# Gated linear attention in a two-layer transformer block: a later wait for the matrix, and the last heads' norm taken by PSUM banks

## The chip, the cores and the metric

The kernel runs on one core of one Trainium2 chip. The metric is the device time of one execution in microseconds. Five engines share the work: TensorE (PE) multiplies matrices into PSUM, VectorE (DVE) and ScalarE (ACT) work element by element, GpSimd (POOL) does what is left over, and SyncE (SP) issues most transfers. They run their own instruction streams and wait for one another through semaphores.

## The reference

Two layers of a transformer block over 1,024 latent and 256 context tokens, all in fp32. Each layer mixes the tokens in three ways (gated linear attention, differential attention, sliding-window attention), projects the mix, and runs a feed-forward block. The change concerns the first of the three, with 4 heads of 64 channels, computed forwards and backwards, summed, and closed by a norm and a gate:

```python
def gla_output(o, og, g):
    bsz, nh, n, dv = o.shape
    on = rms_norm(jnp.moveaxis(o, 1, 2), g)          # x * rsqrt(mean(x^2) + eps) * g, per head
    return (on * jax.nn.silu(og.reshape(bsz, n, nh, dv))).reshape(bsz, n, nh * dv)
...
        gla_lat = gla_output(ol_f + ol_b, pl['go'], gla_norm_g[layer])
```

Layer 0 needs the result for context and latent tokens, layer 1 for the latent ones alone.

## The kernel before, in words

`gated_linear_attention` (from L1284) runs once a layer as a phase of its own; a phase ends when all five instruction streams have ended, and the next (differential attention, from L2236) begins behind it. The 1,280 tokens are 10 chunks of 128 columns; `ASKED` are the chunks whose output is wanted: all 10 in layer 0, the 8 latent ones (2 to 9) in layer 1. One PSUM bank holds 512 columns, four chunks, so the chunks 0 to 3, 4 to 7, and 8 to 9 lie in three banks.

TensorE's work is a list of *units* (`order`, L1345 to L1364), each filling one of the two slots of the PSUM tensor `U` (three banks each) in turn. For each head: transposed keys, the diagonal, the states, seven *levels* of a block-wise attention matrix, and the output. Each entry names the engine that empties the unit, and `slot` (L1505) lets TensorE begin a unit when the unit before the last has been emptied. ScalarE copies the levels 0 and 1 into the matrix `A`, VectorE the diagonal and, under a mask, the levels 2 to 6 (L1790). `S` holds the states, one for each chunk and direction (L1780).

`output(h)` on TensorE (L1555) waits until ScalarE has copied level 1 and VectorE level 6, that is, until `A` is whole; then it clears the unit by a product with zeros (L1561), adds the state products of both directions (L1568, L1575), and last the products of `A` with the values (L1580):

```python
            def output(h):
                s = slot(("output", h))
                pe.wait_ge(act_took, taken(("level", h, 1)))
                pe.wait_ge(dve_took, taken(("level", h, len(LEVELS) - 1)))
```

The heads are normed in pairs. For a pair `i`, ScalarE copies the second head's output out of PSUM into `out` (L1658) and squares it (L1702); TensorE takes the mean of the squares over each head's 64 rows, two columns for each chunk (`mean`, L1588); ScalarE takes the root (L1696), VectorE the reciprocal (L1800); TensorE spreads each reciprocal over 64 rows and the chunk's columns (`root`, L1597); VectorE, which has multiplied `out` by the gate meanwhile (L1796), multiplies it by the spread (L1805); SyncE stores the pair (L1443). For pair 0 all this stands among head 2's levels. For pair 1 nothing is left to stand beside it. `DP` are two further banks, used by the distances (L1501, L1502) until head 3's levels. Every fp32 matmul of the program is two instructions in the profile.

The next phase starts with the score products of its first head (L2349), whose operands were loaded during gated linear attention; VectorE there first waits for the landing of both stores (`gla_stored`, L2514).

Of the kernel before, what the change touches and what calls it, by code (L numbers as in the profile page):

```python
# [18 lines left out]
ALU = mybir.AluOpType  # L19
ACT = mybir.ActivationFunctionType  # L20
AX = mybir.AxisListType

P = 128
# [1260 lines left out]
def gated_linear_attention(nc, t, res, layer, tiles):  # L1284


    with nc.cleanup_on_exit(), ExitStack() as ctx:
# [47 lines left out]
        unit_done, act_took, dve_took, bank_left = sem("unit_done"), sem("act_took"), sem("dve_took"), sem("bank_left")  # L1335
        silu_done, gate_ready, squared, rs_done, og_done = (
            sem("silu_done"), sem("gate_ready"), sem("squared"), sem("rs_done"), sem("og_done"))
        block = ctx.enter_context(nc.Block())
        proj = t["proj"]
        order, taker = [], []  # L1340

        def plan(name, engine, takes):
            order.append(name)
            taker.append((engine, takes))
        for g in range(NS):  # L1345
# [10 lines left out]
            else:  # L1356
# [3 lines left out]
                    plan(("mean", 0), "act", 1)  # L1360
                if h == 2 and p == 4:
                    plan(("root", 0), "dve", 1)
        for name, engine in ((("output", H - 1), "act"), (("mean", 1), "act"), (("root", 1), "dve")):
            plan(name, engine, 1)  # L1364
        at = {name: n for n, name in enumerate(order)}

        def taken(name):
            engine = taker[at[name]][0]
            return sum(k for e, k in taker[:at[name] + 1] if e == engine)

        def left(name):
            return sum({"keys": 1, "diagonal": 1, "output": 4}.get(x[0], 0) for x in order[:at[name]])

        def made(name):
            return at[name] + 1
# [29 lines left out]
        def chunk(c):  # L1405
            return slice(c * P, (c + 1) * P)
# [6 lines left out]
        @block.sync  # L1413
        def _(sp):
            def gates(h):
                load_gates(sp, t, h, ghi[h % 2][:, :, :], glo[h % 2][:, :, :], g_in[h])

            def keys_and_queries(h):
                load_keys_and_queries(sp, t, h, kq[h % 2], kq_in[h % 2])

            sp.dma_start(V[:, :, :], t["vals"][0:T, V_GLA:V_GLA + 2 * P].rearrange("(c p) f -> p c f", p=P)).then_inc(load["v"], 16)
            sp.dma_start(masks[:, :, :], t["gla_masks"]).then_inc(load["mask"], 16)
            sp.dma_start(block_mean[:, :], t["block_mean"]).then_inc(load["bm"], 16)
            for half in range(2):
# [12 lines left out]
            load_differential_constants(sp, t, res["early"], layer)  # L1437
            load_differential_queries(sp, t, res["early"]["queries"], tiles[0] * P, res["early"]["q_in"])
            for h in range(EARLY_HEADS):
                load_differential_keys(sp, t, res["early"]["keys"][:, 2 * h:2 * h + 2, :], h, res["early"]["k_in"][h])  # L1440
            for i in range(2):
                sp.wait_ge(dve_took, taken(("root", i)))
                sp.dma_start(t["mix"][i * P:(i + 1) * P, t0:], out[:, i, t0:]).then_inc(stored, 16)  # L1443

        @block.gpsimd
# [41 lines left out]
        def _(pe):  # L1487
# [66 lines left out]

            def output(h):  # L1555
                s = slot(("output", h))
                pe.wait_ge(act_took, taken(("level", h, 1)))
                pe.wait_ge(dve_took, taken(("level", h, len(LEVELS) - 1)))
                rows = slice(HALF * (h % 2), HALF * (h % 2) + HALF)
                for t0, tn in ((0, BANK), (BANK, BANK), (2 * BANK, T - 2 * BANK)):  # L1560
                    pe.matmul(U[:, s, t0:t0 + tn], zero[:, 0:P], zero[:, 0:tn], start=True, stop=False, skip_group_check=True)  # L1561
                fence = left(("output", h))
                for k in range(NA):
                    f, b = C0 + k, C0 + (k + NA // 2) % NA
                    if f in (4, 8):
                        pe.wait_ge(bank_left, fence + ((2 if C0 else 1) if f == 4 else 3))
                    if f > 0:
                        mm = pe.matmul(U[rows, s, chunk(f)], S[UP, h % 2, f, :], XAB[UP, h % 2, 0, chunk(f)],  # L1568
                                       start=False, stop=False, skip_group_check=True)
                        if f in (3, 7):  # L1570
                            mm.then_inc(bank_left, 1)
                    if b in (C0, 4):
                        pe.wait_ge(bank_left, fence + ((1 if C0 else 2) if b == C0 else 4))
                    if b != 1:
                        mm = pe.matmul(U[rows, s, chunk(b)], S[DOWN, h % 2, BACK.index(b), :], XAB[DOWN, h % 2, 1, chunk(b)],  # L1575
                                       start=False, stop=False, skip_group_check=True)
                        if b in (7, 9):
                            mm.then_inc(bank_left, 1)
                for c in ASKED:
                    mm = pe.matmul(U[rows, s, chunk(c)], V[:, c, h * HALF:(h + 1) * HALF], A[:, h % 2, c, :], start=False, stop=True, skip_group_check=True)  # L1580
                mm.then_inc(unit_done, 1)

            def mean(i):
                s = slot(("mean", i))
                pe.wait_ge(squared, i + 1)
                pe.wait_ge(load["bm"], 16)
                for c in ASKED:
                    mm = pe.matmul(U[:, s, 2 * c:2 * c + 2], square[:, chunk(c)], block_mean[:, 0:P:HALF], start=True, stop=True)  # L1588
                mm.then_inc(unit_done, 1)

            def root(i):
                s = slot(("root", i))
                pe.wait_ge(rs_done, i + 1)
                for c in ASKED:
                    for half, rows in enumerate((UP, DOWN)):
                        spread = rs[:, i, 2 * c + half:2 * c + half + 1].to_broadcast([P, HALF])
                        mm = pe.matmul(U[rows, s, chunk(c)], spread, ident[:, :], start=True, stop=True)  # L1597
                mm.then_inc(unit_done, 1)
# [31 lines left out]
                        root(0)  # L1630
                distances(g + 2, 4)
            output(H - 1)
            mean(1)
            root(1)

        @block.scalar
        def _(act):
# [17 lines left out]
            def take_output(h):  # L1655
                act.wait_ge(unit_done, made(("output", h)))
                rows = slice(HALF * (h % 2), HALF * (h % 2) + HALF)
                act.activation(out[rows, h // 2, t0:], U[rows, at[("output", h)] % 2, t0:T], ACT.Copy, scale=0.125).then_inc(act_took, 1)  # L1658
# [48 lines left out]
            for g in range(NS):  # L1707
# [21 lines left out]
                if h == 0 and p == 4:  # L1729
                    act.wait_ge(load["go"], 16)  # L1730
                    act.activation(go[:, :, :], go[:, :, :], ACT.Silu).then_inc(silu_done, 1)
            take_output(H - 1)
            squares(1)
            take_mean(1)

        @block.vector
        def _(dve):
# [70 lines left out]
            for g in range(NS):  # L1808
# [24 lines left out]
                    reciprocals(0)  # L1833
                if h == 2 and p == 4:
                    take_root(0)
            gate_output(1)
            reciprocals(1)
            take_root(1)

# [1613 lines left out]
```

## Time and profile before

| | us |
|---|---|
| median of 3 runs | 3616.13 (3611.66 to 3618.82) |
| profiled execution, own time | 3619.33 |
| its span in the trace | 3617.4 |
| TensorE busy | 3397.8 (94%) |
| mean granted TensorE clock | 0.967 of full speed |

All times in the rows are microseconds from the start of the span, unless marked ns. The granted clock is 1.00 at 2.4 GHz and 0.50 at 1.2 GHz. In a row of the timeline, `x20` are twenty instructions merged, and the bracket gives the engine's idle time before them and who ended it. PE is TensorE's products, SPq a transfer issued by SyncE.

### The profile page before, as it was taken

The numbers are of one execution on the slowest core, as the hardware profiler recorded it, in microseconds if no ns is written. First come the engines' busy times: TensorE is split into PE (matmuls) and PEld (weight loads), VectorE is DVE, ScalarE is ACT, GpSimd is POOL, SyncE is SP. The second block draws the span as 40 slices with busy tenths as digits, with TensorE's granted clock in tenths as the row PEclk, the third lists the DMA queues.
The fourth block names the chain that finished last, engine by engine and source line by source line (L and its number), as shares of the span: only waits on it lengthen the run. The fifth ranks groups of instructions, "written<-read, shape, count | busy, mean of one in ns | idle before, by whom it ended". The sixth has DMA issues, their size and how long they took to land. (4 is left out here: it accounts for less than half of the span.)

```text
span 3617.4 us, 52096 instructions
## 1 busy us (share of the span) xinstructions
PE 3397.8 (94%) x20432; PEld 2812.0 (78%) x20432; DVE 1643.0 (45%) x2521; ACT 1463.9 (40%) x2355; POOL 1671.9 (46%) x1017
## 2 busy tenths in 40 slices
PE   4999897989999999999999999888898999999998
PEld 4988885666688888888888888886666788888886
DVE  4046545856553322125443317548665441225534
ACT  4151764855443311113343342658654442222222
POOL 3111443943444444445666211338634365556654
PEclk8999996999999999999999999999999999999999
DMA  5244421266532121223333335521455323233322
GB/s 213 88 138 162 123 52 52 53 175 201 168 110 72 64 93 64 70 65 105 122 108 102 112 118 181 151 47 55 96 187 163 111 93 124 98 99 122 106 99 88
DMA packets 207488, 402.54 MB, mean 111 GB/s; under 512 B 19840, under 2 KB 114400, under 8 KB 206752
## 3 DMA queue, kind: packets, MB, share of 16 engines
q1 hardware_dynamic: 185200, 373.88, 32.7%
q10 hardware_dynamic: 20480, 21.32, 1.8%
q0 software_dynamic: 1584, 4.24, 0.4%
q8 instruction: 155, 2.54, 0.3%
q14 instruction: 69, 0.57, 0.0%
HBM read 328.06 MB, written 71.32 MB: 110 GB/s over the span
## 5 line engine op out<-in xcount | busy, mean ns | idle before, releaser
L2907 POOL TENSOR_TENSOR ffn_wlo<-ring_raw,ffn_whi 128x1024 fp32r<-128x1024 f32 x130 | 330.7, 2546 | 306.0 <-ACT ffn_whi L2764 305.7
L2907 POOL TENSOR_TENSOR outproj_ffn_wlo<-ring_raw,outproj_ffn_whi 128x1024 fp32r<-128x1024 f32 x130 | 329.7, 2538 | 303.9 <-ACT outproj_ffn_whi L2764 303.9
L3160 DVE TENSOR_TENSOR ffn_silu<-banks,ffn_silu 128x512 f32<-128x512 f32 x110 | 70.1, 637 | 608.6 <-PE banks L135 608.6
L133 PE MATMUL banks<-second_uhi,ffn_whi 128*128 128x512 f32 (+1 forms) x880 | 325.2, 370 | 1.4 <-POOL ffn_wlo L2907 1.4
L133 PE MATMUL banks<-second_uhi,outproj_ffn_whi 128*128 128x512 f32 (+1 forms) x880 | 324.6, 369 | 2.0 <-PEq L398 2.0
L134 PE MATMUL banks<-second_ulo,ffn_whi 128*128 128x512 f32 (+1 forms) x880 | 324.4, 369 | 0.0
L135 PE MATMUL banks<-second_uhi,ffn_wlo 128*128 128x512 f32 (+1 forms) x880 | 324.2, 368 | 0.0
L134 PE MATMUL banks<-second_ulo,outproj_ffn_whi 128*128 128x512 f32 (+1 forms) x880 | 323.9, 368 | 0.0
L135 PE MATMUL banks<-second_uhi,outproj_ffn_wlo 128*128 128x512 f32 (+1 forms) x880 | 323.7, 368 | 0.0
L2764 ACT CAST ffn_whi<-ring_raw 128x1024 fp32r<-128x1024 f32 x132 | 138.0, 1048 | 325.0 <-PE banks L135 211.8
L2764 ACT CAST outproj_ffn_whi<-ring_raw 128x1024 fp32r<-128x1024 f32 x130 | 135.9, 1049 | 328.1 <-PE banks L135 193.0
L2772 ACT ACTIVATE ffn_silu<-banks 128x512 f32<-128x512 f32 x110 | 61.0, 555 | 456.5 <-PE banks L135 455.8
L2488 DVE TENSOR_SCALAR_CACHE_REDUCE diff_scores<-diff_scores 128x1280 f32<-128x1280 f32 (+1 forms) x144 | 196.7, 1383 | 24.1 <-PE diff_scores L2349 19.2
L3176 DVE TENSOR_TENSOR y<-banks,y 128x512 f32<-128x512 f32 x200 | 138.1, 691 | 133.6 <-PE banks L135 133.6
L2466 POOL TENSOR_TENSOR diff_w<-diff_w,diff_e 128x1280 f32<-128x1280 f32 (+1 forms) x72 | 192.0, 2667 | 6.0
L2022 POOL TENSOR_SCALAR swa_p<-swa_p,swa_rden 128x640 f32<-128x640 f32 (+1 forms) x144 | 107.3, 763 | 189.0 <-DVE swa_rden L2204 189.0
L2418 ACT ACTIVATE diff_e<-diff_scores,diff_negmax 128x1280 f32<-128x1280 f32 (+1 forms) x144 | 178.2, 1238 | 37.6 <-DVE diff_scores L2488 36.8
L133 PEld LDWEIGHTS banks<-second_uhi,outproj_ffn_whi 128*128 128x128 f32 x880 | 165.9, 189 | 30.3 <-issue 2.8
L133 PEld LDWEIGHTS banks<-second_uhi,ffn_whi 128*128 128x128 f32 x880 | 166.3, 189 | 29.6 <-POOL ffn_wlo L2907 1.8
L135 PEld LDWEIGHTS banks<-second_uhi,ffn_wlo 128*128 128x128 f32 x880 | 166.2, 189 | 27.9
L134 PEld LDWEIGHTS banks<-second_ulo,ffn_whi 128*128 128x128 f32 x880 | 166.4, 189 | 27.4
L135 PEld LDWEIGHTS banks<-second_uhi,outproj_ffn_wlo 128*128 128x128 f32 x880 | 165.9, 188 | 27.7
(375 smaller groups left out, 8892.7 us busy)
## 6 DMA issues: line engine op xcount, KB each, us to landing
ring_raw<-w_ffn_dram SPq DMA_DIRECT2D x264, 512.0 KB
swa_ada_w<-w_ada_dram SPq DMA_DIRECT2D x20, 2048.0 KB
local_qhl<-heads_scratch SPq DMA_DIRECT2D x36, 256.0 KB, 8.3
outproj_mix<-mix_scratch SPq DMA_DIRECT2D x18, 512.0 KB, 4.5
first_ada_w<-w_ada_dram SPq DMA_DIRECT2D x4, 2048.0 KB
outproj_wraw<-w_out_dram SPq DMA_DIRECT2D x8, 1024.0 KB, 9.7
in_w_raw<-w_in_dram SPq DMA_DIRECT2D x15, 512.0 KB, 5.7
heads_scratch<-in_vAhi SPq DMA_DIRECT2D x12, 640.0 KB, 3.0
```

The source lines that it names most:

```text
L133: pe.matmul(out, st_hi, mv_hi, start=start, stop=False)
L134: pe.matmul(out, st_hi, mv_lo, start=False, stop=False)
L135: return pe.matmul(out, st_lo, mv_hi, start=False, stop=stop)
L2022: pool.tensor_scalar(pr[:, m % RING, j, 0:keys], pr[:, m % RING, j, 0:keys], rden[:, m % RING, j:j + 1], 1.0, ALU.mult, ALU.mult).then_inc ...
L2418: act.activation(E[:, r % 4, c, 0:keys], SC[:, c, 0:keys], ACT.Exp, bias=ng[:, c:c + 1], scale=-1.0, accum_out=den[:, c, tile_of(i, r), r ...
L2466: pool.tensor_tensor(w, w, E[:, u % 4, 0, 0:keys], ALU.add).then_inc(w_done, 1)
L2488: dve.tensor_scalar(SC[:, c, 0:keys], SC[:, c, 0:keys], -scale, 3e38, ALU.mult, ALU.min, accum_out=ng[:, c:c + 1]).then_inc(neg_done, 1)
L2764: act.copy(whi(w), raw[:, w % 2, :]).then_inc(w_hi, 1)
L2772: act.activation(sg[:, n % 2, 0:tn], GT[:, n % 2, 0:tn], ACT.Silu).then_inc(silu_done, 1)
L2907: pool.tensor_tensor(wlo(w), raw[:, w % 2, :], whi(w).bitcast(F32), ALU.subtract).then_inc(w_ready, 1)
L3160: dve.tensor_tensor(sg[:, n % 2, 0:tn], UP[:, n % 2, 0:tn], sg[:, n % 2, 0:tn], ALU.mult).then_inc(mul_done, 1)
L3176: dve.tensor_tensor(Y(tt)[:, cols], accumulators(q, n)[:, half, :], Y(tt)[:, cols], ALU.add).then_inc(y_added, 1)
```

## The change

It has three parts. `output(h)` waits for the states before it clears the unit, and for `A` behind the state products. The last head's output and the second pair's norm are taken out of the unit order and done by banks: `BY_BANK` holds the asked chunks of each bank (4, 4, 2 in layer 0; 2, 4, 2 in layer 1), and copy, square, mean, root, gate, reciprocal, spread and scaling are each issued three times on these parts, interleaved by hand on each engine, with six new semaphores. The means go to the two banks of `DP`, the spreads to the other slot of `U`. ScalarE takes a root of one column of constants ahead of the last copies. The store waits for the third scaling and stays one transfer.

```diff
+        BY_BANK = [[c for c in ASKED if c * P // BANK == n] for n in range(3)]
+        plan(("output", H - 1), "act", len(BY_BANK))
-        for name, engine in ((("output", H - 1), "act"), (("mean", 1), "act"), (("root", 1), "dve")):
-            plan(name, engine, 1)
...
+        sums, spreads = U[:, at[("output", H - 1)] % 2, :], U[:, 1 - at[("output", H - 1)] % 2, :]
@@ SyncE
-                sp.wait_ge(dve_took, taken(("root", i)))
+                if i == 0:
+                    sp.wait_ge(dve_took, taken(("root", 0)))
+                else:
+                    sp.wait_ge(scaled, len(BY_BANK))
@@ TensorE, output(h)
                 s = slot(("output", h))
-                pe.wait_ge(act_took, taken(("level", h, 1)))
-                pe.wait_ge(dve_took, taken(("level", h, len(LEVELS) - 1)))
+                pe.wait_ge(dve_took, taken(("states", h)))
...
-                for c in ASKED:
-                    mm = pe.matmul(U[rows, s, chunk(c)], V[...], A[:, h % 2, c, :], ...)
-                mm.then_inc(unit_done, 1)
+                pe.wait_ge(act_took, taken(("level", h, 1)))
+                pe.wait_ge(dve_took, taken(("level", h, len(LEVELS) - 1)))
+                for part in BY_BANK:
+                    for c in part:
+                        mm = pe.matmul(U[rows, s, chunk(c)], V[...], A[:, h % 2, c, :], ...)
+                    if h == H - 1:
+                        mm.then_inc(weighed, 1)
+                if h < H - 1:
+                    mm.then_inc(unit_done, 1)
+            def last_mean(n):
+                pe.wait_ge(squared, n + 2)
+                if n == 2:
+                    pe.wait_ge(rooted, 1)
+                for k, c in enumerate(BY_BANK[n]):
+                    mm = pe.matmul(DP[:, n % 2, 2 * k:2 * k + 2], square[:, chunk(c)], block_mean[:, 0:P:HALF], ...)
+                mm.then_inc(mean_done, 1)
+            def last_spread(n):
+                pe.wait_ge(inv_done, n + 1)
+                for c in BY_BANK[n]:
+                    for half, rows in enumerate((UP, DOWN)):
+                        mm = pe.matmul(spreads[rows, chunk(c)], rs[:, 1, 2 * c + half:2 * c + half + 1].to_broadcast([P, HALF]), ident[:, :], ...)
+                mm.then_inc(spread_done, 1)
...
             output(H - 1)
-            mean(1)
-            root(1)
+            last_mean(0); last_mean(1); last_spread(0); last_mean(2); last_spread(1); last_spread(2)
@@ ScalarE
-            take_output(H - 1)
-            squares(1)
-            take_mean(1)
+            def last_output(n):
+                cols = columns(BY_BANK[n])
+                act.wait_ge(weighed, n + 1)
+                act.activation(out[DOWN, 1, cols], sums[DOWN, cols], ACT.Copy, scale=0.125).then_inc(act_took, 1)
+                act.wait_ge(act_took, taken(("output", H - 1)) - len(BY_BANK) + n + 1)
+                act.activation(square[:, cols], out[:, 1, cols], ACT.Square).then_inc(squared, 1)
+            def last_root(n):
+                act.wait_ge(mean_done, n + 1)
+                act.activation(sd[:, 1, heads_of(part)], DP[:, n % 2, 0:2 * len(part)], ACT.Sqrt, bias=eps[:, 0:1]).then_inc(rooted, 1)
+            act.activation(sd[:, 1, 0:1], eps[:, :], ACT.Sqrt)
+            act.wait_ge(unit_done, made(("mean", 0)))
+            last_output(0); last_output(1); last_root(0); last_output(2); last_root(1); last_root(2)
@@ VectorE
-            gate_output(1)
-            reciprocals(1)
-            take_root(1)
+            last_gate(n):    wait squared n + 2;  out *= go on the bank's columns             -> og_done
+            last_inverse(n): wait rooted n + 1;   rs = 1 / sd on the bank's columns           -> inv_done
+            last_scaling(n): wait spread_done n + 1, og_done n + 2; out *= spreads            -> scaled
+            last_gate(0); last_gate(1); last_inverse(0); last_gate(2); last_inverse(1)
+            last_scaling(0); last_inverse(2); last_scaling(1); last_scaling(2)
```

The calls in a row stand on lines of their own in the kernel, and VectorE's three functions are given by what they wait for and do.

## Rows read from the trace of the kernel before

**Rows 1.** The page: busy time of each engine, share of the span, instructions.
```profile
PE 3397.8 (94%) x20432; PEld 2812.0 (78%) x20432; DVE 1643.0 (45%) x2521; ACT 1463.9 (40%) x2355; POOL 1671.9 (46%) x1017
```

**Rows 2.** Timeline, layer 0's end: start us, us, engine, line, operation, out<-in, count [idle before].
```profile
545.47 1.60 DVE L1790 COPY_PREDICATED gla_A<-gla_masks,gla_unit 128x1280 f32<-128x1280 int32 x1 [0.29 <-PE gla_unit L1552]
...
547.75 0.28 PE L1552 MATMUL gla_unit<-gla_X,gla_XK 128*128 128x128 f32 x1
548.06 1.57 DVE L1790 COPY_PREDICATED gla_A<-gla_masks,gla_unit 128x1280 f32<-128x1280 int32 x1 [1.00 <-PE gla_unit L1552]
549.78 0.82 PE L1561 MATMUL gla_unit<-gla_zero 128*128 128x512 f32 x3 [1.76 <-DVE gla_A L1790]
...
554.19 2.73 PE L1580 MATMUL gla_unit<-gla_A,gla_V 128*64 128x128 f32 x20
556.96 1.23 ACT L1658 ACTIVATE early_mixed<-gla_unit 64x1280 f32<-64x1280 f32 x1 [11.54 <-PE gla_unit L1580]
558.22 1.27 ACT L1702 ACTIVATE head_lv<-early_mixed 128x1280 f32<-128x1280 f32 x1
559.51 1.28 ACT L1696 ACT_TABLE_LOAD   x1
559.59 2.45 PE L1588 MATMUL gla_unit<-gla_block_mean,head_lv 128*128 128x2 f32 x20 [2.67 <-issue]
...
562.39 0.28 DVE L1800 RECIPROCAL gla_rs<-gla_sd 128x20 f32<-128x20 f32 x1 [1.32 <-ACT gla_sd L1696]
562.81 4.53 PE L1597 MATMUL gla_unit<-ident,gla_rs 128*64 128x128 f32 x40 [0.77 <-DVE gla_rs L1800]
567.38 1.49 DVE L1805 TENSOR_TENSOR early_mixed<-early_mixed,gla_unit 128x1280 f32<-128x1280 f32 x1 [4.72 <-PE gla_unit L1597]
568.90 0.34 SPq L1443 DMA_DIRECT2D mix_scratch<-early_mixed  x1
```

**Rows 3.** Timeline, layer 1's end, the same relay; TensorE and the store.
```profile
2417.75 5.75 PE L1552 MATMUL gla_unit<-gla_X,gla_XK 128*128 128x128 f32 x48 [0.31 <-DVE gla_X L1760]
...
2424.97 0.82 PE L1561 MATMUL gla_unit<-gla_zero 128*128 128x512 f32 x3 [1.47 <-DVE gla_A L1790]
...
2428.19 1.96 PE L1580 MATMUL gla_unit<-gla_A,gla_V 128*64 128x128 f32 x16
...
2432.39 3.54 PE L1588 MATMUL gla_unit<-gla_block_mean,head_lv 128*128 128x2 f32 x16 [2.24 <-issue]
...
2441.65 0.34 SPq L1443 DMA_DIRECT2D mix_scratch<-early_mixed  x1
```

**Rows 4.** Timeline, layer 0: head 0's output, and the first pair's spread.
```profile
417.67 0.74 PE L1561 MATMUL gla_unit<-gla_zero 128*128 128x512 f32 x3
...
420.77 2.40 PE L1580 MATMUL gla_unit<-gla_A,gla_V 128*64 128x128 f32 x20
...
508.06 2.40 PE L1597 MATMUL gla_unit<-ident,gla_rs 128*64 128x128 f32 x40
```

**Rows 5.** Small copies on the timeline; squares and last scaling by line (ns min/median/max).
```profile
2407.79 0.58 ACT L1675 COPY gla_A<-gla_unit 64x512 f32<-64x512 f32 x1 [0.42 <-PE gla_unit L1552]
...
2411.92 0.36 ACT L1675 COPY gla_A<-gla_unit 32x256 f32<-32x256 f32 x1 [0.62 <-PE gla_unit L1552]
...
L1702 ACT ACTIVATE head_lv<-early_mixed x4: 1056/1164/1269, 478.6 to 2431.2; 128x1280 f32<-128x1280 f32 x2, 128x1024 f32<-128x1024 f32 x2
...
L1805 DVE TENSOR_TENSOR early_mixed<-early_mixed,gla_unit x4: 1220/1356/1489, 510.5 to 2440.4; 128x1280 f32<-128x1280 f32 x2, 128x1024 f32<-128x1024 f32 x2
```

**Rows 6.** Windows: stretch, us, busy of PE PEld DVE ACT POOL (xcount), PEclk, DMA.
```profile
551.50:554.80 3.30, 3.30 (x27) 2.97 (x26) 0.00 (x0) 0.00 (x0) 0.00 (x0) 0.50 0.00 0
562.90:567.30 4.40, 4.40 (x40) 4.04 (x40) 0.00 (x0) 0.00 (x0) 0.00 (x0) 0.50 0.01 4
...
2432.50:2435.90 3.40, 3.40 (x16) 3.35 (x16) 1.11 (x1) 1.09 (x1) 0.00 (x0) 0.50 0.00 0
```

**Rows 7.** Timeline, VectorE's first work of the phase behind, layer 0.
```profile
572.39 0.43 DVE L2488 TENSOR_SCALAR_CACHE_REDUCE diff_scores<-diff_scores 128x256 f32<-128x256 f32 x1 [3.51 <-DMA mix_scratch<-early_mixed]
```

More of the change, by code:

```diff
@@ L1337, in gated_linear_attention @@
             sem("silu_done"), sem("gate_ready"), sem("squared"), sem("rs_done"), sem("og_done"))
+        weighed, mean_done, rooted, inv_done, spread_done, scaled = (
+            sem("weighed"), sem("mean_done"), sem("rooted"), sem("inv_done"), sem("spread_done"), sem("scaled"))
         block = ctx.enter_context(nc.Block())
@@ L1369, in taken, with columns, heads_of @@
             return sum(k for e, k in taker[:at[name] + 1] if e == engine)
+        def columns(part):
+            return slice(part[0] * P, (part[-1] + 1) * P)
+        def heads_of(part):
+            return slice(2 * part[0], 2 * part[-1] + 2)
+        sums, spreads = U[:, at[("output", H - 1)] % 2, :], U[:, 1 - at[("output", H - 1)] % 2, :]
         def left(name):
@@ L1578, in output @@
                             mm.then_inc(bank_left, 1)
-                for c in ASKED:
-                    mm = pe.matmul(U[rows, s, chunk(c)], V[:, c, h * HALF:(h + 1) * HALF], A[:, h % 2, c, :], start=False, stop=True, skip_group_check=True)
-                mm.then_inc(unit_done, 1)
+                pe.wait_ge(act_took, taken(("level", h, 1)))
+                pe.wait_ge(dve_took, taken(("level", h, len(LEVELS) - 1)))
+                for part in BY_BANK:
+                    for c in part:
+                        mm = pe.matmul(U[rows, s, chunk(c)], V[:, c, h * HALF:(h + 1) * HALF], A[:, h % 2, c, :], start=False, stop=True, skip_group_check=True)
+                    if h == H - 1:
[7 more added lines that the diff above has]
+                for k, c in enumerate(BY_BANK[n]):
+                    mm = pe.matmul(DP[:, n % 2, 2 * k:2 * k + 2], square[:, chunk(c)], block_mean[:, 0:P:HALF], start=True, stop=True)
+                mm.then_inc(mean_done, 1)
[3 more added lines that the diff above has]
+                    for half, rows in enumerate((UP, DOWN)):
+                        mm = pe.matmul(spreads[rows, chunk(c)], rs[:, 1, 2 * c + half:2 * c + half + 1].to_broadcast([P, HALF]), ident[:, :], start=True, stop=True)
+                mm.then_inc(spread_done, 1)
             def mean(i):
@@ L1632, in _ @@
             output(H - 1)
-            mean(1)
-            root(1)
+            last_mean(0)
+            last_mean(1)
+            last_spread(0)
+            last_mean(2)
+            last_spread(1)
+            last_spread(2)
         @block.scalar
@@ L1731, in _ @@
                     act.activation(go[:, :, :], go[:, :, :], ACT.Silu).then_inc(silu_done, 1)
-            take_output(H - 1)
-            squares(1)
-            take_mean(1)
+            def last_output(n):
[5 more added lines that the diff above has]
+            def last_root(n):
+                part = BY_BANK[n]
+                act.wait_ge(mean_done, n + 1)
+                act.activation(sd[:, 1, heads_of(part)], DP[:, n % 2, 0:2 * len(part)], ACT.Sqrt, bias=eps[:, 0:1]).then_inc(rooted, 1)
+            act.activation(sd[:, 1, 0:1], eps[:, :], ACT.Sqrt)
+            act.wait_ge(unit_done, made(("mean", 0)))
+            last_output(0)
+            last_output(1)
+            last_root(0)
+            last_output(2)
+            last_root(1)
+            last_root(2)
         @block.vector
@@ L1835, in _, with last_gate, last_inverse, last_scaling @@
                     take_root(0)
-            gate_output(1)
-            reciprocals(1)
-            take_root(1)
+            def last_gate(n):
+                cols = columns(BY_BANK[n])
+                dve.wait_ge(squared, n + 2)
+                dve.tensor_tensor(out[:, 1, cols], out[:, 1, cols], go[:, 1, cols], ALU.mult).then_inc(og_done, 1)
+            def last_inverse(n):
+                part = BY_BANK[n]
+                dve.wait_ge(rooted, n + 1)
+                dve.reciprocal(rs[:, 1, heads_of(part)], sd[:, 1, heads_of(part)]).then_inc(inv_done, 1)
+            def last_scaling(n):
+                cols = columns(BY_BANK[n])
+                dve.wait_ge(spread_done, n + 1)
+                dve.wait_ge(og_done, n + 2)
+                dve.tensor_tensor(out[:, 1, cols], out[:, 1, cols], spreads[:, cols], ALU.mult).then_inc(scaled, 1)
+            last_gate(0)
+            last_gate(1)
+            last_inverse(0)
+            last_gate(2)
+            last_inverse(1)
+            last_scaling(0)
+            last_inverse(2)
+            last_scaling(1)
+            last_scaling(2)
 def local_buffers(nc, ctx, layer):
```

## The prediction

> **What bounds the kernel now.** First the page's busy line: TensorE is busy 94% of the span [rows 1], so time is mostly lost where TensorE waits. The change touches only gated linear attention, so the second view is the timeline of its end in each layer [rows 2, 3]. The reader is to see a relay: after the last level's products, one engine at a time works. In layer 0 the last level's products end at 548.03 (547.75 + 0.28); VectorE copies them into the matrix, 548.06 to 549.63; only then does TensorE clear the unit and begin the last head's output (549.78, idle 1.76). The matrix products end at 556.92; ScalarE copies and squares; TensorE takes the mean, 559.59 to 562.04; the root with its hand-offs costs 0.35 us, the reciprocal 0.28; TensorE spreads, 562.81 to 567.34; VectorE scales; SyncE issues the store at 568.90, the phase's last work. Layer 1 runs the same relay from 2423.50 (2417.75 + 5.75) to 2441.65 [rows 3]. From the last level's products to the store it is **20.87 us in layer 0 and 18.15 us in layer 1**, and nothing else covers it.
>
> The third thing to see is the clock. At 2.4 GHz, head 0's output took 3.10 us from clearing to the matrix products (417.67 to 420.77) and 2.40 us for 20 of these; 40 spread instructions took 2.40 [rows 4]. In layer 0's last output the granted clock fell to 0.50, 1.2 GHz, after TensorE's idle 1.76 us, and it was 0.50 in layer 0's spreads and in layer 1's mean [rows 6]. So 7.14 us were paid (549.78 to 556.92) where head 0 paid 5.50, and 0.113 us a spread instruction where 0.06 is possible.
>
> **The change part by part.** *The moved wait.* The output now waits for the states alone before clearing, and for the matrix only before the matrix products. What still holds its start is the PSUM slot, last read by the copy of the level before: that copy ended at 547.07 (545.47 + 1.60) [rows 2], before the last level's products. So TensorE starts at once and the last copy (1.57 us) hides beneath 3.1 us of clearing and state products. Removed: 1.76 us in layer 0, 1.47 in layer 1 [rows 2, 3], and, as no idle time precedes it, I take layer 0's output at head 0's price. If the cover were gone, the idle time would be back. For heads 0 to 2 I take nothing: the same order stands there, and head 0's clearing had no idle time in front [rows 4]. Behind the two waits on TensorE's queue stand the matrix products, which need that data anyway.
>
> *The last output bank by bank.* Layer 0's banks hold 4, 4 and 2 chunks, layer 1's 2, 4 and 2. Prices: a copy of 64x512 0.58 us and of 256 columns 0.36; squares of 1280 and 1024 columns take 1.27 and 1.06, so 0.63 for 512 and 0.42 for 256; VectorE's products 1.49 and 1.22, so 0.68 and 0.41 [rows 5]. A chunk is two instructions of matrix or mean products at 0.12 us each (20 in 2.45 us for the mean) [rows 2] and four of spreads at 0.06 [rows 4]. Hand-offs to TensorE cost 0.14 (562.67 to 562.81), others 0.03 or 0.04 [rows 2].
>
> Layer 0, counted from the end of the last level's products: matrix products begin at 3.2; the first bank's 8 are done, with 0.15 for filling, at 4.3; two copies and two squares on ScalarE with hand-offs (2.55) reach 6.85; the second bank's mean (0.14 + 0.98) 7.97; the first bank's spread (0.1 + 16 x 0.06) 9.03; the third mean 9.56; the second spread 10.57; the third 11.1. Beside that the second scaling runs 10.6 to 11.3 and the third ends at 11.7. The store's issue comes at 11.75 instead of 20.87: **9.1 us less.** Covered are the third copy and square, the roots and the gate products; the nearest miss is the first reciprocal, ready at 7.9 where it is needed at 7.97.
>
> Layer 1: matrix products begin at 3.27 (3.22 in [rows 3]); banks are done at 3.76, 4.75 and 5.23; first copy and square to 4.6; second to 6.03; second mean 7.15; spreads and the last mean to 9.8; last scaling 10.4; store at 10.45 instead of 18.15: **7.7 us less.** The sum at 2.4 GHz is 16.8.
>
> *What the clock gives back.* From the first mean on TensorE has short gaps, and the mean has only two columns; layer 1's mean ran at 0.50 before [rows 6]. At 0.50 a mean instruction takes 0.22 (16 in 3.54) [rows 3] and a spread 0.113 [rows 2]. From the second mean on that adds, in layer 0, 0.8 + 0.85 + 0.4 + 0.85 + 0.42 less 0.15 that the scalings absorb, 3.2; in layer 1, with 0.42 for its first spread, 2.75. So the sum lies between 16.8 and 10.9. Before, the clock was at 0.50 before either tail ended [rows 6], but the idle stretches ahead of that fall are gone; a fall somewhere within the spreads lies between the two, and I take the middle: **13.8 us less.**
>
> *Small edits.* The early root (1.28 + 0.28 us) fills ScalarE's idle 11.54 us before the last copy [rows 2]; uncovered it would cost 1.56 a layer. Its wait for the first pair's mean was met long ago. The reciprocals on fewer columns keep their 0.28. SyncE's store waits for three scalings and stays one DMA; nothing stands behind it on that queue but the phase's end. No DMA moves, and POOL's queue is untouched. TensorE's new waits are not shown before: their cost lies between nothing and the mean's own late start, taken here as at most 0.3 us for each of six groups a layer, 3.6 us in all; I take the 0.14 row, since it is a TensorE wait for a semaphore, and keep 3.6 for the range. Six more semaphores beside the 28 of the phase I put at nothing: the 3.5 us from the store's issue (568.90) to VectorE's next work (572.39) end with the store's landing [rows 2, 7]; in proportion six would be 0.6 us a layer, an estimate, kept for the range.
>
> *Tables.* One load a layer stands in the tail, 1.28 us, 0.02 behind the square's end (558.22 + 1.27, load at 559.51) [rows 2]. Squares have so far run under the exponential's table with no load in the row [rows 5]. After the change they run behind the root's. If the root's table has no Square, four more loads a layer stand in ScalarE's chain (before the first square, the first root, the third square, the second root): 8 x 1.28 = 10.2 us back. I take none, with that as a rival.
>
> The Trainium skill (ScalarE: Activation LUTs, Table sets: the hidden batching unit) speaks against this order: calls should be batched by set, and it names relu, copy, identity and abs as present in every set, not Square. Its section What ACT_TABLE_LOAD costs prices a switch at about 2.66 us with a drain; by that the eight would cost 21.3 us and the change would lose 7.5. The trace has the drain nowhere: the load behind the square starts 0.02 us after it [rows 2].
>
> **Profile and median.** The profiled execution took 3619.33 us, span 3617.4 and 1.9 around it; minus 13.8 is 3605.5. It stands 3.2 above the median of 3616.13, so the forecast is **3602.3**. A difference of 0.2% is 7.2 us, about what a measurement of this kernel can tell from none.
>
> **Rivals.**
> *Tables switch (0.09).* As above: 13.8 less 10.2, so 3.6 us faster, 3612.5. For it: no row shows Square behind a root. Against: copies and Square share the exponential's table, as functions of every set would.
>
> *The start doesn't move (0.04).* If the PSUM slot holds clearing until the last copy after all, the 1.76 and 1.47 stay, and layer 0's fall of the clock with them (7.14 less 5.50): 4.9 back, 8.9 faster, 3607.2. Against it: the slot's reader ended at 547.07.
>
> *Swallowed behind the phase (0.05).* The next phase might be held by what doesn't move. VectorE waits there for the landing of this very store (3.51 us) [rows 7], which moves along; a load begun earlier that landed later would hold it. Then 0 to 5 us faster, about 3614.
>
> *Hand-offs dear (0.03), the other side.* The relay grows to about nine hand-offs a layer in the chain. Were each of these 18 to cost over 0.77 us beyond its row, the gain is gone; at 1.2 us it is 7.8 us slower, 3623.9. Rows show 0.03 to 0.15, so this would need waits on TensorE to stall its queue in a way no row shows.
>
> **How the numbers follow.** The forecast has 0.79. Its own range is 3599.3 (all at 2.4 GHz) to 3608.8 (half clock and dear waits: 10.9 less 3.6). Some 2 to 3 us of scatter between runs (the three span 7.2) widen it below to 3597; above, most of the tables' rival is taken in: 3611. Faster by over 0.2%: 0.76 of the forecast and most of the second rival, 0.79. Within 0.2%: tables, swallowed and the forecast's rest, 0.17. Slower: 0.04.
>
> **What the profile would show.** Right: clearing within 0.1 us of the last level's products, no idle time behind VectorE's last copy; three copies and three squares, the second bank's matrix products running beneath the first copy; one table load a layer, early; store 11.8 and 10.5 us behind the last level's products, up to 15 and 13 if the clock falls. The granted clock of the spreads decides between 16.8 and 10.9. Wrong: loads between squares and roots; TensorE idle over 0.5 us before each spread; or an earlier store with the differential phase starting no earlier or finishing at the old time.

## The result, and the profile after

The changed kernel takes **3596.25 us** (median of 4 runs, 3595.64 to 3598.51) beside 3613.89 us for the kernel before (4 runs, 3610.98 to 3618.82): a ratio of 0.995, 95% interval 0.9936 to 0.9964. That is 17.6 us less. The forecast was 3602.3 us, in a range whose lower end was 3597.0: the sign and the relay's new shape came out as predicted, the size was larger, and the median lies 0.75 us below the range. The profiled execution of the changed kernel took 3598.51 us, its span is 3596.3.

The first thing to read is layer 0's end, the stretch that [rows 2] show of before. The fence is the timeline of the changed kernel, with the same columns; left out are weight loads, the state products and lines that repeat the pattern for another bank.

```profile
539.83 5.33 PE L1565 MATMUL gla_unit<-gla_X,gla_XK 128*128 128x128 f32 x43
...
542.57 1.28 ACT L1781 ACT_TABLE_LOAD   x1
...
544.92 0.83 PE L1573 MATMUL gla_unit<-gla_zero 128*128 128x512 f32 x3
545.20 1.59 DVE L1844 COPY_PREDICATED gla_A<-gla_masks,gla_unit 128x1280 f32<-128x1280 int32 x1 [1.01 <-PE gla_unit L1565]
...
548.11 2.40 PE L1595 MATMUL gla_unit<-gla_A,gla_V 128*64 128x128 f32 x20
549.29 0.59 ACT L1772 ACTIVATE early_mixed<-gla_unit 64x512 f32<-64x512 f32 x1 [5.22 <-PE gla_unit L1595]
549.91 0.63 ACT L1774 ACTIVATE head_lv<-early_mixed 128x512 f32<-128x512 f32 x1
...
551.19 0.63 ACT L1774 ACTIVATE head_lv<-early_mixed 128x512 f32<-128x512 f32 x1
551.85 0.27 ACT L1779 ACTIVATE gla_sd<-gla_dist,gla_eps 128x8 f32<-128x8 f32 x1
...
551.87 1.05 PE L1606 MATMUL gla_dist<-gla_block_mean,head_lv 128*128 128x2 f32 x8 [0.22 <-ACT head_lv L1774]
...
552.55 0.42 ACT L1774 ACTIVATE head_lv<-early_mixed 128x256 f32<-128x256 f32 x1
552.86 1.09 PE L1613 MATMUL gla_unit<-ident,gla_rs 128*64 128x128 f32 x16
...
553.88 0.61 PE L1606 MATMUL gla_dist<-gla_block_mean,head_lv 128*128 128x2 f32 x4
...
554.42 1.53 PE L1613 MATMUL gla_unit<-ident,gla_rs 128*64 128x128 f32 x24
...
556.60 0.34 SPq L1456 DMA_DIRECT2D mix_scratch<-early_mixed  x1
...
560.05 0.43 DVE L2564 TENSOR_SCALAR_CACHE_REDUCE diff_scores<-diff_scores 128x256 f32<-128x256 f32 x1 [3.48 <-DMA mix_scratch<-early_mixed]
```

Three things stand there. Clearing (L1573) begins at 544.92, while the last level's products still drain (they end at 545.16, the first row: 539.83 + 5.33), and VectorE's last copy runs beneath it: the idle 1.76 us of [rows 2] is gone. The relay has become an overlap: the second bank's square ends at 551.82, its mean starts 0.05 later, and the first spread follows it without an idle row. And the store is issued at 556.60, **11.44 us** behind the last level's products instead of 20.87 [rows 2].

Layer 1 is the same relay, to be held against [rows 3]. The last level's products end at 2410.56 (2404.82 + 5.74) and the store is issued at 2421.14: **10.58 us** instead of 18.15. What differs from layer 0, beside the order of the banks (2, 4 and 2 chunks), is a longer wait ahead of the second bank's mean, 0.41 us, and TensorE's last row: the 24 spreads take 2.09 us where layer 0's take 1.53.

```profile
2404.82 5.74 PE L1565 MATMUL gla_unit<-gla_X,gla_XK 128*128 128x128 f32 x48 [0.30 <-DVE gla_X L1814]
2410.32 0.83 PE L1573 MATMUL gla_unit<-gla_zero 128*128 128x512 f32 x3
...
2413.55 1.96 PE L1595 MATMUL gla_unit<-gla_A,gla_V 128*64 128x128 f32 x16
...
2416.45 1.05 PE L1606 MATMUL gla_dist<-gla_block_mean,head_lv 128*128 128x2 f32 x8 [0.41 <-ACT head_lv L1774]
...
2418.56 2.09 PE L1613 MATMUL gla_unit<-ident,gla_rs 128*64 128x128 f32 x24
...
2421.14 0.34 SPq L1456 DMA_DIRECT2D mix_scratch<-early_mixed  x1
```

Why, the windows say: stretch, its length, busy time of PE, PEld, DVE, ACT and POOL with counts, and then the granted clock, which [rows 6] had at 0.50 in three stretches of these tails. In layer 0 it is 1.00 through means and spreads. In layer 1 it falls, but only in the last spreads.

```profile
551.50:553.50 2.00, 1.78 (x22) 1.68 (x23) 1.30 (x4) 1.65 (x5) 0.00 (x0) 1.00 0.00 0
553.50:556.00 2.50, 2.45 (x38) 2.02 (x32) 1.34 (x4) 0.26 (x1) 0.00 (x0) 1.00 0.00 0
...
2417.00:2419.20 2.20, 2.20 (x29) 2.00 (x30) 1.35 (x6) 1.04 (x4) 0.00 (x0) 1.00 0.00 0
2419.20:2420.70 1.50, 1.45 (x18) 1.05 (x12) 0.70 (x2) 0.00 (x0) 0.00 (x0) 0.56 0.00 0
```

The two tails together are 9.43 + 7.57 = 17.0 us shorter, and the medians 17.6 us apart. What lies behind the phase moves along: VectorE's first work of the next phase still comes behind the store's landing, with an idle stretch of 3.48 us (the last row of the first fence) where [rows 7] have 3.51.

The page's busy line hardly moves: TensorE is busy for 94% as before, 3388.1 us instead of 3397.8 [rows 1] with the same count of instructions. So the 9.7 us less are no work left out: the same products ran at the higher clock for more of the time. Of the 9.7, 6.4 lie in the two tails, where TensorE is busy for 20.1 us instead of 26.4 (10.47 + 9.59 against 14.12 + 12.31) and the mean granted clock rises from 0.75 and 0.74 to 1.00 and 0.92. ScalarE and VectorE have 14 and 12 instructions more and are each about as busy as before.

```profile
PE 3388.1 (94%) x20432; PEld 2801.9 (78%) x20432; DVE 1652.2 (46%) x2533; ACT 1467.0 (41%) x2369; POOL 1670.9 (46%) x1017
```

### The profile page after: what moved, and what is told of

It reads as the page before. It is cut to its first block and busy times, and to the rows that moved or that the text cites. A ratio compares the mean times of both kernels' runs of the same rounds, so it can differ in the third digit from the quotient of the medians.

```text
span 3596.3 us, 52130 instructions
## 1 busy us (share of the span) xinstructions
PE 3388.1 (94%) x20432; PEld 2801.9 (78%) x20432; DVE 1652.2 (46%) x2533; ACT 1467.0 (41%) x2369; POOL 1670.9 (46%) x1017
```

## The experiments

"Tail" is the time from the end of the last level's products to the issue of the second pair's store. Ratios are against the kernel before, timed on the same chip; they and their intervals are taken from the single runs, and the quotient of the two medians lies up to 0.0008 below the ratio.

| run | tail, layer 0 | tail, layer 1 | median us | ratio (95%) |
|---|---|---|---|---|
| kernel before | 20.87 | 18.15 | 3613.89 | |
| changed kernel | 11.44 | 10.58 | 3596.25 | 0.995 (0.9936 to 0.9964) |
| the same again | 11.43 | 10.53 | 3596.68 | 0.9961 (0.9947 to 0.9975) |
| moved wait alone | 17.58 | 14.47 | 3609.25 | 0.9991 (0.9982 to 1.0001) |
| banks alone | 14.43 | 11.89 | 3602.17 | 0.9971 (0.996 to 0.9982) |
| tables switched | 17.03 | 16.20 | 3607.16 | 0.999 (0.9981 to 1.0) |
| no early root | 13.55 | 12.46 | 3603.38 | 0.9975 (0.9964 to 0.9986) |
| means three times | 19.42 | 16.40 | 3612.74 | 1.0 (0.9991 to 1.001) |
| store's wait later | 11.45 | 10.88 | 3595.38 | 0.996 (0.9946 to 0.9973) |

The kernel before had a median of 3613.29 us over 27 runs beside the first four experiments and of 3612.70 over 18 beside the last three.

### The changed kernel once more

No edit. It asks whether the good clock of the first trace was luck.

> The changed kernel itself, once more, for the size of the gain and for a second trace of its clock. Theory (the term for the clock was too large, the rest of the sum was right): tails within 1 us of 11.44 and 10.58, the granted clock 1.00 up to the last spreads again, and 17.0 us below before by the tails. Rival (where the clock falls differs from execution to execution, and the first trace was a lucky one): spreads at 0.113 us an instruction in at least one layer, a tail there of 13 to 14.5 us.

Measured: tails of 11.43 and 10.53 us, the clock at 1.00 through layer 0's tail, and in layer 1 a fall inside the last 24 spreads, which take 2.05 us. The two traces agree to 0.05 us in either tail. The profiled times, 3598.51 and 3592.86, lie 5.7 us apart all the same: the rest of the program scatters by that much, the tails do not. So the tails are the sharper measure for everything below.

### The moved wait alone

The kernel before, with `output(h)` waiting for the states ahead of clearing and for the matrix ahead of its products; the norm is left as it was.

```diff
                 s = slot(("output", h))
-                pe.wait_ge(act_took, taken(("level", h, 1)))
-                pe.wait_ge(dve_took, taken(("level", h, len(LEVELS) - 1)))
+                pe.wait_ge(dve_took, taken(("states", h)))
...
+                pe.wait_ge(act_took, taken(("level", h, 1)))
+                pe.wait_ge(dve_took, taken(("level", h, len(LEVELS) - 1)))
                 for c in ASKED:
```

> The kernel before with the moved wait alone; the last heads' norm stays whole. Measured by the tail, from the end of the last level's products to the store's issue (before: 20.87 us in layer 0, 18.15 in layer 1). Theory (the clock falls behind TensorE's idle stretches, and both of the wait's gaps are gone): the last output of layer 0 takes 5.5 us at a granted clock of 1.00, so layer 0's tail is 17.5 and layer 1's 16.7; the whole kernel 4.9 us below before. Rival (the fall of the clock in layer 0's output has nothing to do with the gap ahead of it): 19.1 and 16.7, 3.2 us below before.

Measured: 17.58 us in layer 0, the theory's 17.5; layer 1's tail is 14.47, 2.2 shorter than expected. The trace shows both. The first three rows are the timeline of this kernel, the next two its windows.

```profile
543.42 0.83 PE L1560 MATMUL gla_unit<-gla_zero 128*128 128x512 f32 x3
546.60 2.40 PE L1581 MATMUL gla_unit<-gla_A,gla_V 128*64 128x128 f32 x20
...
2421.91 1.92 PE L1589 MATMUL gla_unit<-gla_block_mean,head_lv 128*128 128x2 f32 x16 [2.24 <-issue]
```
```profile
551.60:553.40 1.80, 1.73 (x16) 1.76 (x16) 1.49 (x1) 1.27 (x1) 0.00 (x0) 1.00 0.00 0
553.60:554.40 0.80, 0.78 (x4) 0.69 (x4) 0.00 (x0) 0.00 (x0) 0.00 (x0) 0.50 0.00 0
```

Layer 0's output runs at head 0's price: from clearing to the end of the matrix products it is 5.58 us, against 5.50 in [rows 4] and 7.14 before. So the idle time does go, and the half clock in the output goes with it. In layer 0 the fall now sits inside the mean, at 553.5, and the 40 spreads still take 4.54 us at half clock; that the tail meets 17.5 to 0.1 is in part luck, since clearing starts 0.24 us earlier than counted and the mean takes 0.26 us longer than before. In layer 1 the mean, 3.54 us before at half clock [rows 3], takes 1.92. The total moved by 4.0 us beside 7.0 us of tails, and the interval reaches to 6.5 us only (0.9982). In the trace nothing behind the tails takes the gain back: from layer 0's store to layer 1's last level it is 1853.5 us beside 1854.6 before, and from layer 1's store to the end 1175.3 beside 1175.8. Where the medians lose the 3 us was not settled.

### The banks alone

The changed kernel, with the wait for the matrix back ahead of clearing.

```diff
                 s = slot(("output", h))
-                pe.wait_ge(dve_took, taken(("states", h)))
+                pe.wait_ge(act_took, taken(("level", h, 1)))
+                pe.wait_ge(dve_took, taken(("level", h, len(LEVELS) - 1)))
...
-                pe.wait_ge(act_took, taken(("level", h, 1)))
-                pe.wait_ge(dve_took, taken(("level", h, len(LEVELS) - 1)))
                 for part in BY_BANK:
```

> The changed kernel with the wait for the matrix put back ahead of the clearing; copy, square, mean, root, spread and scaling stay by banks. Theory (the two parts add): the tails of the changed kernel, 11.44 and 10.58 us, grow by the idle 1.76 and 1.47 us to 13.2 and 12.05, the clock holds, and the whole is 13.8 us below before. Rival (the gap brings the clock down as it did before, and the relay by banks then runs at 0.50): layer 0 about 18.0 (1.6 more in the output, 3.2 more in means and spreads), layer 1 14.8, together 6.2 us below before.

Measured: tails of 14.43 and 11.89, 11.1 us off the median, between the theory's 13.8 and the rival's 6.2. Layer 1 is the theory's 12.05 to 0.2 us, in part by luck (counted from the last level's products, clearing comes 1.7 us later than in the changed kernel, and the last spreads are 0.56 us shorter); layer 0 lies between the two, 1.2 above the theory. The timeline and a window of this kernel:

```profile
543.35 0.82 PE L1574 MATMUL gla_unit<-gla_zero 128*128 128x512 f32 x3 [1.76 <-DVE gla_A L1843]
...
552.83 2.70 PE L1612 MATMUL gla_unit<-ident,gla_rs 128*64 128x128 f32 x24
...
2421.17 1.53 PE L1612 MATMUL gla_unit<-ident,gla_rs 128*64 128x128 f32 x24
```
```profile
552.80:555.50 2.70, 2.70 (x25) 2.31 (x25) 1.17 (x3) 0.26 (x1) 0.00 (x0) 0.54 0.00 0
```

The idle 1.76 us is back, and in layer 0 the last 24 spreads take 2.70 instead of 1.53 us at a granted clock of 0.54. Without the moved wait clearing starts 1.76 us behind the last level's products instead of 0.24 ahead of their end, 2.0 us, and the last spreads take 1.17 us more; of these 3.2 the tail shows 3.0. So in layer 0 the two gains nearly add up (3.29 and 6.44 alone, 9.43 together). In layer 1 the banks alone already escape the half-clock mean that the moved wait alone also escapes, so there the two gains overlap (3.68 and 6.26 alone, 7.6 together).

### Tables switched

The changed kernel, with an exponential of one column, whose result nothing reads, ahead of the first and third squares. It forces the exponential's table in, so that the next root has to load its own again: the rival of the prediction, built.

```diff
+                if n != 1:
+                    act.activation(spare[:, :], eps[:, :], ACT.Exp)
                 act.activation(square[:, cols], out[:, 1, cols], ACT.Square).then_inc(squared, 1)
```

> The changed kernel with an exponential of one column (its result is not used) ahead of the first and the third square, so that ScalarE must change its table four more times a layer: before each of these, before the first and before the second root. It prices the rival of the prediction that a Square without a place in the root's table would have cost. By this case's rows a change costs 1.28 us and nothing more: with the two exponentials' 0.2 us, 5.5 us a layer if all of it is on the path, tails of at most 16.9 and 16.1 us, and the kernel still at least 6 us below before. By the Trainium skill's page ScalarE: Activation LUTs, section What ACT_TABLE_LOAD costs, a change costs 2.66 us: tails of 22.5 and 21.6 us, and the kernel some 4 us above before.

Measured: tails 5.6 and 5.7 us longer than the changed kernel's in its second trace, 0.1 us above the bounds of 16.9 and 16.1, and the median 10.5 us above it. The timeline of layer 0 in this kernel:

```profile
548.03 0.59 ACT L1773 ACTIVATE early_mixed<-gla_unit 64x512 f32<-64x512 f32 x1 [5.22 <-PE gla_unit L1596]
548.64 1.28 ACT L1776 ACT_TABLE_LOAD   x1
549.94 0.20 ACT L1776 ACTIVATE gla_spare<-gla_eps 128x1 f32<-128x1 f32 x1
550.05 0.61 ACT L1777 ACTIVATE head_lv<-early_mixed 128x512 f32<-128x512 f32 x1
...
551.95 1.28 ACT L1782 ACT_TABLE_LOAD   x1
...
553.81 1.97 PE L1614 MATMUL gla_unit<-ident,gla_rs 128*64 128x128 f32 x16 [0.77 <-DVE gla_rs L1901]
...
555.79 1.01 PE L1607 MATMUL gla_dist<-gla_block_mean,head_lv 128*128 128x2 f32 x4
...
557.61 2.83 PE L1614 MATMUL gla_unit<-ident,gla_rs 128*64 128x128 f32 x24 [0.81 <-DVE gla_rs L1901]
```

A switch costs 1.28 us: the load starts 0.02 behind the copy and the next function 0.02 behind the load. Four of them are 5.1 us, but not all of that is in the tail's chain. Held against the changed kernel row by row, loads, dummies and the waits for them lengthen layer 0's tail by about 3.0 us; the other 2.6 are half clock, in the 16 spreads (1.97 us instead of 1.09), the four products of the third mean (1.01 instead of 0.61) and the 24 spreads (2.83 instead of 1.53). In layer 1 it is about 4.0 and 1.6. So that 5.6 lies near four loads is luck. In the changed kernel these loads are absent: three squares and three roots run behind the one load at 542.57, so Square has a place in the root's table, and here a square runs right behind an exponential (549.94, 550.05), so it has one in that table too. The Trainium skill (ScalarE: Activation LUTs, What ACT_TABLE_LOAD costs) puts 2.66 us on a switch, half of it a drain; this trace agrees on the load, 1.28, and shows no drain.

### No early root

The changed kernel without ScalarE's root of a constant column (`act.activation(sd[:, 1, 0:1], eps, ACT.Sqrt)`), so that the table is loaded at the first real root.

> The changed kernel without ScalarE's early root of one column. Theory: the load of the root's table then stands ahead of the first root, where the first inverse is not needed until the second mean is done, so of its 1.28 us part lies beside TensorE's second mean and part delays ScalarE's third copy and with it the third square: tails longer by 0.5 to 1.3 us each (12.0 to 12.7 and 11.1 to 11.8), total 1 to 2.6 us above the changed kernel. Rival (the early root is worth nothing, the load is hidden either way): tails unchanged within 0.2 us, total the same.

Measured: tails of 13.55 and 12.46 us, 2.1 and 1.9 longer, more than the theory's 1.3. Layer 0's timeline and a window:

```profile
548.17 1.28 ACT L1779 ACT_TABLE_LOAD   x1
...
550.02 1.09 PE L1613 MATMUL gla_unit<-ident,gla_rs 128*64 128x128 f32 x16 [0.76 <-DVE gla_rs L1897]
...
551.72 2.83 PE L1613 MATMUL gla_unit<-ident,gla_rs 128*64 128x128 f32 x24
```
```profile
551.80:554.50 2.70, 2.70 (x24) 2.34 (x24) 0.91 (x3) 0.26 (x1) 0.00 (x0) 0.50 0.00 0
```

TensorE waits 0.76 us for the first reciprocal: part of the load lies beside the second mean, as the theory had it. The rest is the clock: the 16 spreads behind that wait still run at 1.00, then it falls to 0.50, and the last 24 take 2.83 instead of 1.53 us. So one instruction of 0.2 us is worth 2 us a layer. That the wait itself brings the fall is not shown: in layer 1 the clock falls as far behind the last level's products here as in the changed kernel (8.5 and 8.8 us), and the wait has moved more of the spreads behind that point. The total rose by 6.7 us between two medians, 2.7 more than the tails; the intervals of the two ratios overlap, and where those 2.7 us are was not settled.

### The means three times

The changed kernel, each of the last three means' products issued three times over, with the same result.

```diff
-                for k, c in enumerate(BY_BANK[n]):
+                for k, c in [x for x in enumerate(BY_BANK[n]) for _ in range(3)]:
```

> The changed kernel, with each product of the last three means issued three times in a row (the same result written thrice), so that TensorE spends three times as long on two-column products in the tail. It tells whether such products by themselves pull TensorE's clock down, as the prediction's half of the clock's price supposed. Theory (they do not; only idle stretches ahead do): the granted clock of layer 0 stays at 1.00 through the second mean, a mean product stays at 0.12 us, so the second mean grows by 1.96 us, the third by 0.98, the first by about 1.5 of its 1.96 (the rest lies beside ScalarE's second copy and square): layer 0's tail goes from 11.43 to about 15.9, layer 1's (4, 8 and 4 products) from 10.55 to about 13.7, and the total is some 7.5 us above the changed kernel. Rival (they do): the clock falls to 0.50 inside the second mean, a mean product takes 0.22 and a spread 0.113 from there on, layer 0's tail reaches 20 us or more and layer 1's 17 or more, and the total is 15 us above.

Measured: 19.42 and 16.40, and a median back at that of the kernel before. That is 0.6 us short of the rival's 20 and 17 and far above the theory's 15.9 and 13.7. The timeline row merges the first two means, and the windows show the clock.

```profile
550.33 6.18 PE L1606 MATMUL gla_dist<-gla_block_mean,head_lv 128*128 128x2 f32 x48
```
```profile
550.30:554.80 4.50, 4.47 (x40) 4.47 (x41) 2.01 (x4) 2.29 (x5) 0.00 (x0) 1.00 0.00 0
555.00:558.00 3.00, 3.00 (x24) 2.98 (x23) 0.20 (x1) 0.27 (x1) 0.00 (x0) 0.50 0.00 0
558.00:564.00 6.00, 5.83 (x40) 5.08 (x38) 1.68 (x4) 0.26 (x1) 0.00 (x0) 0.50 0.00 0
```

The theory, that only an idle stretch ahead takes the clock down, falls. Forty mean products run at 1.00 with no idle row among them, and behind them the clock is 0.50 to the tail's end. So the prediction's reason for charging the clock was not empty. In layer 0 the fall comes 10.1 us behind the last level's products, where the changed kernel has none before 13.5. But the means need not be what brings it: the tails with the moved wait alone, with the tables switched and without the early root fall at 9.9 us with no longer means, and in layer 1 the fall is at 8.5 us here and at 8.8 in the changed kernel.

### The store's wait moved

The changed kernel, with VectorE's wait for the landing of the stores put ahead of its first write that needs it, instead of at the start of the next phase. It asks whether the 3.48 us are time of the kernel.

```diff
+                    if isinstance(i, int) and i == first_pair and u == 0:
+                        dve.wait_ge(early["gla_stored"], 32)
                     dve.wait_ge(pv_done, done(i, u))
...
-            dve.wait_ge(early["gla_stored"], 32)
```

> The changed kernel, with VectorE's wait for the landing of gated linear attention's stores moved from the start of the next phase to just ahead of the first write that needs it. It tells whether those 3.5 us behind the store are time of the kernel or only of VectorE. Theory (TensorE there waits for other things, so nothing is gained): VectorE's 3.5 us idle stretch is gone or shorter, the differential phase's later work starts where it did, total within 1 us of the changed kernel. Rival (VectorE's wait holds TensorE): 1.4 us or more a layer is gained, 3 us or more in total, and this version beats both kernels.

Measured: 3595.38 us, a ratio of 0.996 beside the changed kernel's 0.9961 in its second comparison. The timeline of this kernel:

```profile
558.39 0.43 DVE L2564 TENSOR_SCALAR_CACHE_REDUCE diff_scores<-diff_scores 128x256 f32<-128x256 f32 x1 [1.99 <-PE diff_scores L2425]
...
567.34 0.79 PE L2425 MATMUL diff_scores<-diff_k,early_queries 96*128 96x256 f32 x2 [3.15 <-DMA diff_k<-heads_scratch]
```

VectorE's stretch shrinks from 3.48 to 1.99 us, and TensorE then waits longer for the keys of the next heads: 3.15 us, where the second trace of the changed kernel has 2.40. That product with the keys, whose load the new phase itself issues, stands 10.9 us behind the store's issue here and 10.7 and 11.0 in the two traces of the changed kernel. The wait changed its name, and no version here was shown to beat the changed kernel.

## Why the prediction came out short

**The step that failed** is "What the clock gives back". It charged 3.0 us, the middle between 16.8 at 2.4 GHz and 10.9 with the clock at 0.50 from the second mean on. Measured in the changed kernel: nothing in layer 0 and 2.09 less 1.53 = 0.56 us in layer 1. The tails shortened by 17.0 us, the prediction's own sum at 2.4 GHz to 0.2. The relay was read rightly, this term was mis-sized: it put the fall as early as the second mean because [rows 6] show layer 1's mean at 0.50.

What the runs show instead is that in layer 1 the fall hardly moved, while the work moved ahead of it. These are windows of the kernel before, the changed kernel, the moved wait alone and the means three times, each the one in which layer 1's clock falls:

```profile
2432.00:2432.50 0.50, 0.11 (x1) 0.14 (x1) 0.12 (x1) 0.48 (x2) 0.00 (x0) 0.73 0.00 0
2419.00:2419.50 0.50, 0.50 (x12) 0.50 (x10) 0.14 (x1) 0.00 (x0) 0.00 (x0) 0.87 0.00 0
2423.70:2424.20 0.50, 0.13 (x2) 0.04 (x1) 0.03 (x1) 0.27 (x1) 0.00 (x0) 0.82 0.00 0
2425.00:2426.00 1.00, 1.00 (x9) 1.00 (x8) 0.00 (x0) 0.00 (x0) 0.00 (x0) 0.75 0.00 0
```

Counted from the end of the last level's products, these falls come at 8.7, 8.8, 9.3 and 8.5 us, and eight of the nine traces have layer 1's fall between 8.5 and 9.3; in the ninth, the banks alone, there is none before the store. Before, the whole mean and all the spreads stood behind that point; in the changed kernel 1.8 us of the tail do. In layer 0 the three traces that hold the whole change keep 2.4 GHz until 13.5 us or later, when the tail is over. Why the fall comes where it does stays open, and whether the idle stretches that the change removes had brought it about before is not shown.

**The second share is the starting point.** The forecast was set off from 3616.13, the median of three runs; with more runs the kernel before has 3613.89, 3613.29 and 3612.70. Of the 6.05 us between forecast and result, 3.2 are the clock's term (17.0 less 13.8), 2.2 the median (3616.13 less 3613.89), and 0.6 is what the medians moved beyond the tails (17.6 less 17.0). A miss by either alone would have stayed inside the range.

**What held.** Moved wait: clearing starts at once, the copy hides beneath it, and layer 0's output costs 5.59 us (544.92 to 550.51) where 5.50 was taken; shown by the moved wait alone. Bank by bank: in layer 0 the second mean ends 7.76 us behind the last level's products (7.97 predicted), the last spread at 10.79 (11.1), the store at 11.44 (11.75); nearly the whole lead is that the matrix products began at 2.95 instead of 3.2. Layer 1's store came at 10.58 (10.45), with the half-clock spreads in it. New waits on TensorE: 0.22 us of idle time before the second mean in layer 0 and 0.41 in layer 1, and none ahead of the spreads: more than the 0.14 taken for a hand-off, and far from the 0.77 of the rival on the other side. Early root: it lies in ScalarE's idle time, over at 544.07 where the first copy starts at 549.29; taking it out cost 2.1 and 1.9.

**The rivals.** Tables switch: refuted, there is one load a layer. Forced, it cost 10.5 us where 10.2 was worked out, but that is a sum of partly covered loads and half clock. The start doesn't move: refuted, no idle row ahead of clearing. Swallowed: refuted; VectorE's stretch behind the store is the same 3.5 us, and the gain of the tails reaches the end. Hand-offs dear: refuted.

**Left open.** In the pair of profiled executions the kernels lie 20.8 us apart, 3.8 more than the tails. Of these, 2.9 lie ahead of layer 0's tail, whose last level ends at 548.03 before and at 545.16 after. The moved wait in heads 0 to 2 is not needed for that: with the banks alone, which leave the work ahead of the tail as it was, it ends at 541.59. The clock of the first 100 us, 0.83 before and 0.91 after in a stretch that the change does not touch, does not explain it: without the early root it is 0.83 too, and the last level ends at 541.49. The medians show 0.6 of these 3.8 us, and they are taken as scatter. What decides at which product the clock falls was not settled either.

## What to carry to other kernels

Where a phase ends in a relay, count only the time from the last work that everything shares to the last store: cut into pieces that fit the buffers, here PSUM banks, the relay shortened by about a third with no less work done, and with the moved wait by more than two fifths. Wait for an operand where it is read, and load a table while its engine is idle anyway. When a clock fall may or may not hit the new stretch, don't charge half of it: treat the two ends as cases, and ask how much work will still stand behind the place where it fell before.

## What was not expected of the hardware

The granted clock fell to 0.50 with no idle row of TensorE ahead of it in the tail, inside a row of mean products (means three times, layer 0: 1.00 to 554.80, 0.50 from 555.00). An idle stretch alone does not decide a fall either: with the banks alone, layer 1 has the idle 1.47 us ahead of its output and keeps 2.4 GHz to the last spread (24 in 1.53 us), while the changed kernel has no such stretch there and pays half clock in its last spreads (2.09 and 2.05 us in its two traces). And with a wait of 0.76 us in the middle of layer 0's tail (no early root), the last spreads took 1.30 us longer than without it, more than the wait itself.
